# Storing four residual tiles during the routing and keeping expert 6's gate/up weights in their place

## The reference

```
x = x + mixer(rms_norm(x, g_mix))
x = x + hier_moe(rms_norm(x, g_ffn))

gp   = softmax(h @ w_rg + b_rg)            # 4 expert groups, take the best one
e_w  = top-2 of softmax over its 8 experts, normalised, times the group's share
hg, hu = h @ w_gate[e], h @ w_up[e]        # 32 experts, 1024 -> 256
y    = sum_e (silu(hg) * hu * e_w[e]) @ w_down[e]     # 256 -> 1024
```

## Time and profile before

| | us |
|---|---|
| median of 3 runs | 1165.74 (1164.16 to 1169.99) |
| the profiled execution, its own time | 1167.69 |
| its span | 1165.9 |
| matmuls (PE) busy | 1029.6 (88%) |
| SP's largest group of waits: on its own weight loads at L599 | 265.6 in 44 |
| mean TensorE clock granted, of full speed | 0.95 |

### The profile page before, as it was taken

One profiled execution on the slowest core, in us unless ns is written; L12 is line 12 of the kernel. 1 busy time (PEld: TensorE's weight loads), 2 busy tenths in 40 slices (PEclk: granted clock), 3 DMA queues, 4 the chain that ended last, 5 costly groups with the idle time before them and its releaser, 6 DMA issues.

```text
span 1165.9 us, 19198 instructions
## 1 busy us (share of the span) xinstructions
PE 1029.6 (88%) x7043; PEld 652.8 (56%) x7044; DVE 428.8 (37%) x906; ACT 209.6 (18%) x425; POOL 182.5 (16%) x270
## 2 busy tenths in 40 slices
PE   5999998869889988788389989988998999999980
PEld 4888786545555544344167767654555554555540
DVE  2541002454722111111249899635462121211216
ACT  4000102232201110110140101144120111111112
POOL 1000010000042221211103120110004222323220
PEclk9999999999999998898799999999988999999995
DMA  9424033345479999999752100264056999999946
GB/s 360 204 102 159 7 119 74 134 192 215 151 251 408 408 409 409 408 409 411 312 212 74 43 31 1 47 233 185 37 211 198 406 406 402 410 406 396 406 184 232
DMA packets 74512, 281.61 MB, mean 242 GB/s; under 512 B 13182, under 2 KB 13886, under 8 KB 71296
## 3 DMA queue, kind: packets, MB, share of 16 engines
q1 hardware_dynamic: 58192, 253.76, 55.7%
q0 software_dynamic: 11120, 17.89, 4.4%
q10 hardware_dynamic: 5120, 8.87, 2.3%
HBM read 270.75 MB, written 29.65 MB: 258 GB/s over the span
## 4 chain that ended last, share of the span: by engine, by line
PE 62%; DMA 21%; DVE 12%; ACT 2%; issue 2%; SPq 0%; POOLq 0%; DVEq 0%; ACTq 0%; POOL 0%
DMA ring<-w_moe 12%; PE psum L2175 12%; PE psum L2079 7%; DMA ar<-w_moe 6%; PE psum L2242 6%; PE psum L1850 6%; PE psum L1806 5%; PE psum L2281 5%; DVE ar L1709 5%; PE psum L2306 3%; PE psum L1919 2%; PE psum L2158 2%; DVE X L1426 2%; PE psum L2207 1%; DMA ring<-expert_outputs 1%
## 5 line engine op out<-in xcount | busy, mean ns | idle before, releaser
L2175 PE MATMUL psum<-ring,ar 128*64 128x256 f32 x1408 | 176.0, 394 | 21.9 <-DMA ring<-w_moe 15.9
L2175 PEld LDWEIGHTS psum<-ring,ar 128*64 128x64 f32 x1408 | 100.9, 141 | 93.8 <-issue 32.6
L2281 PE MATMUL psum<-ar,ring 128*128 128x272 f32 x512 | 121.3, 398 | 5.3 <-DVE ar L1695 2.9
L2281 PEld LDWEIGHTS psum<-ar,ring 128*128 128x128 f32 x512 | 97.6, 192 | 30.2 <-issue 4.2
L1632 DVE COPY ar<-psum 128x128 f32<-128x128 f32 x64 | 18.7, 291 | 247.8 <-PE psum L2232 247.8
L1709 DVE SCALAR_TENSOR_TENSOR ar<-ar,sv 128x512 f32<-128x512 f32 x120 | 106.9, 893 | 5.8 <-ACT ar L1049 1.9
L2079 PE MATMUL psum<-ring,ar 128*128 128x512 f32 x192 | 90.7, 622 | 4.7 <-DVE ar L1411 4.7
L2175 PE MATMUL psum<-ar 128*64 128x256 f32 x640 | 82.9, 404 | 8.2 <-DMA ar<-w_moe 8.2
L2242 PE MATMUL psum<-ring,ar 128*64 128x512 f32 x352 | 84.1, 598 | 0.8 <-DVE ar L1632 0.8
L2175 PEld LDWEIGHTS psum<-ar 128*64 128x64 f32 x640 | 46.2, 144 | 43.0 <-issue 12.9
L973 ACT ACTIVATE ar<-psum 128x128 f32<-128x128 f32 x64 | 17.8, 278 | 288.9 <-PE psum L2175 288.9
(11 more groups left out here) (265 smaller groups left out, 1205.4 us busy)
## 6 DMA issues: line engine op xcount, KB each, us to landing
ring<-w_moe SPq DMA_DIRECT2D x44, 2048.0 KB, 16.6
ring<-w_moe SPq DMA_DIRECT2D x44, 1024.0 KB, 18.6
ar<-w_moe SPq DMA_DIRECT2D x20, 2048.0 KB, 16.7
ar<-w_moe SPq DMA_DIRECT2D x20, 1024.0 KB, 18.3
ring<-w_pw SPq DMA_DIRECT2D x6, 2048.0 KB, 10.8
ring<-w_mix SPq DMA_DIRECT2D x3, 3072.0 KB, 29.3
ring<-expert_outputs SPq DMA_DIRECT2D x6, 1024.0 KB, 9.1
ring<-kv_in SPq DMA_DIRECT2D x2, 2880.0 KB, 11.1
```

The costliest lines, as they stand in the source:

```text
L2175: t = mm(psum[64 * f:64 * f + 64, u % 2, 0:2 * P], xt[:, k, 64 * (u % 2):64 * (u % 2) + 64], w[:, k, f, :], start=k == 0, stop=k == KD - 1)
L2281: t = mm(psum[:, glu_bank(m) + h, 0:HALF], w[:, k, o:o + P], hT2[:, k, HALF * h:HALF * h + HALF], start=k == 0, stop=k == KD - 1)
```

## The change

Four tiles of `X` (4, 2, 3, 0) are stored to a new buffer in memory as soon as they are normed, by ScalarE's queue. When these stores have landed and TensorE has transposed the tiles, SP loads expert 6's four gate/up pieces into the places of tiles 2, 3, 4 and 0, in two transfers, after the preloads of experts 0 to 5. In the first round of the expert loop ScalarE copies one piece into slot 0 after each of `keep_y(1)` to `keep_y(4)`; the fourth copy increments `w_in[0]` by 16, as the load did. The load of expert 6's gate/up in `weights` is left out. The stored tiles are loaded back behind the last expert's down weights, and `combine` waits for them.

```diff
+        x_dram = nc.dram_tensor("residual_rows", (TOK, D), F32, kind="Internal").ap()
 ...
 # SP, experts(n), after the preloads
+                sp.wait_ge(moe.residual, 160 * n + 64)
+                sp.wait_ge(turned, 10 * (2 * n + 1) + 2 * (TILES - 1))
+                for tiles, c in ((slice(2, 5), 0), (slice(0, 1), 3)):
+                    k = tiles.stop - tiles.start
+                    sp.dma_start(X[:, tiles, :], w_moe[n, MSLOTS, c:c + k, :, :].rearrange("c p x -> p c x")
+                                 ).then_inc(moe.residual, 16)
+
-                def weights(it, jobs):
+                def weights(it, jobs, staged=False):
                     for u in range(jobs):
                         sp.wait_ge(moe.gu_free, MSLOTS * it + (EXPERTS * n + u + 1 - MSLOTS))
                         sp.sem_inc(moe.seen, 1)
                         b = (u - 2) % MSLOTS
                         sp.wait_ge(moe.w_in[b], 16 * it + 16 * (loads_before(n, b) + (u >= 2)))
                         e = bass.ds(MSLOTS * it + u, 1)
-                        sp.dma_start(pieces(u)[:, 0:GU, :], ...).then_inc(moe.w_in[u], 16)
+                        if not staged or u:
+                            sp.dma_start(pieces(u)[:, 0:GU, :], ...).then_inc(moe.w_in[u], 16)
                         sp.wait_ge(moe.down_done, MSLOTS * it + (EXPERTS * n + u + 1 - MSLOTS))
                         sp.sem_inc(moe.seen, 1)
                         sp.dma_start(pieces(u)[:, GU:, :], ...).then_inc(moe.w_down_in[u], 16)

-                with sp.Fori(1, EXPERTS // MSLOTS) as it:
+                weights(1, MSLOTS, True)
+                with sp.Fori(2, EXPERTS // MSLOTS) as it:
                     weights(it, MSLOTS)
                 weights(EXPERTS // MSLOTS, EXPERTS % MSLOTS)
+                sp.wait_ge(moe.w_in[0], 16 * (loads_before(n, 0) + 2))
+                for i in (0, 2, 3, 4):
+                    sp.dma_start(X[0:ROWS[i], i, :], x_dram[P * i:P * i + ROWS[i], :]).then_inc(moe.residual, 16)
 ...
 # ScalarE, norm(call), call odd
                         act.dma_start(xn_dram[P * i:P * i + r, :], xn[0:r, :]).then_inc(moe.xn_out[s % 2], 16)
+                        if s < TILES - 1:
+                            act.dma_start(x_dram[P * i:P * i + r, :], X[0:r, i, :]).then_inc(moe.residual, 16)
 ...
 # ScalarE, experts(n)
+                def unstage(c):
+                    act.wait_ge(moe.gu_free, EXPERTS * n + 1)
+                    act.wait_ge(moe.residual, 160 * n + 96)
+                    t = nc.scalar.activation(slot(0)[:, PIECE * c:PIECE * c + PIECE], X[:, (2, 3, 4, 0)[c], :], ACT.Copy)
+                    if c < GU - 1:
+                        link(t)
+                    else:
+                        t.then_inc(moe.w_in[0], 16)
 ...
                         silu(it, u, first)
                         if later(first, u):
                             keep_y(it, u - 1, first)
+                        if first and u >= 2:
+                            unstage(u - 2)
 ...
 # VectorE
             def combine(n):
+                dve.wait_ge(moe.residual, 160 * n + 160)
```

More of the change, by code:

```diff
@@ L298, in __init__ @@
                 self.combined = sem("combined")
+                self.residual = sem("residual")
         class Further:
@@ L598, in weights @@
                         e = bass.ds(MSLOTS * it + u, 1)
-                        sp.dma_start(pieces(u)[:, 0:GU, :], w_moe[n, e, 0:GU, :, :].rearrange("a c p x -> p (a c) x")
-                                     ).then_inc(moe.w_in[u], 16)
+                        if not staged or u:
+                            sp.dma_start(pieces(u)[:, 0:GU, :],
+                                         w_moe[n, e, 0:GU, :, :].rearrange("a c p x -> p (a c) x")
+                                         ).then_inc(moe.w_in[u], 16)
                         sp.wait_ge(moe.down_done, MSLOTS * it + (EXPERTS * n + u + 1 - MSLOTS))
```

## The result

The changed kernel takes 1202.96 us (median of 6 runs, 1198.09 to 1208.42), the one before 1169.64 in the same comparisons: a ratio of 1.0275, 95% interval 1.0238 to 1.0311, that is 32 us slower. The forecast was 1192 against a before of 1165.74, 26 us slower. The profiled execution spans 1198.8 us, 32.9 more than the one of before.

A forecast was written before the change was run, and what follows sets the result against it. The prediction took layer 0's experts as bound by the DMA engines and layer 1's by TensorE. Its terms 12.4 + 4 + 9.6 made 26.0 us, so 1192 against a median of 1165.74, range 1181 to 1202.

The forecast's parts named there:

- What binds and what holds the stream: Layer 0's experts bound by DMA, layer 1's by TensorE; SP's wait on w_in[0] for ScalarE's fourth copy holds later weight loads.
- Staging wins nothing: Expert weight stream: slots, not bytes, hold its start, so leaving out expert 6's load wins at most 1.5 us, taken as 0.
- Layer 0's experts, 12.4: Expert loop of layer 0: expert 8's load lands late and all later loads keep the distance, +12.4 us.
- The landing I took from the earlier trace as 7.8: Expert 8's gate/up load, issued into an empty queue, takes 7.8 us like expert 6's earlier load.
- The copy, 1.15 in the sum: ScalarE's fourth copy, 128x1024, after keep_y(4): 1.15 us, taken from the scaling of a norm.
- The 6.8 us that follow from the fit: Expert 8's 2.1 MB load by the skill page's fit: 6.8 us, one less than the trace row, which was preferred.
- the queue was to be empty by 353: Layer 0's weight queue: loads issued before the hold are through by some 353, then it is empty until 367.35.
- Layer 0's end, 4: After layer 0's experts: the reload adds 4.2 us to the queue and the read-back starts later, +4 us, bounds 1.5 and 6.
- Layer 1, 9.6: Expert loop of layer 1: the same wait makes expert 8's load 12.8 us late, less 3.2 slack, +9.6, bounds 5 and 13.
- The 1 us for a gather lengthened by the staging: Layer 1's start: expert 6's preload may lengthen GpSimd's gather of the first further chunk, +1 us, bounds 0 and 3.
- What costs nothing: Both layers' stores, the first three copies and layer 1's reload are covered by idle time and cost nothing.
- Expert 6's late start: TensorE starts expert 6 in layer 0 at 367.35 instead of 365.22, +2.1 us, the same 2.1 in layer 1.

The follow-up runs named there:

- e1: Changed kernel, but SP does not wait for the landing of expert 6's gate/up before issuing expert 8's: 1182.68 us, ratio 1.0108.
- e2: Kernel before plus one wait only: SP issues expert 8's gate/up after ScalarE's keep_y(4); no stores, staging or reload: 1196.44 us, ratio 1.0225.
- e6: Kernel before with only the wait before expert 8's gate/up, released one expert earlier, after keep_y(3): 1185.00 us, ratio 1.0124.
- e5: Changed kernel with ScalarE's four copies made after experts 1 and 2, and without SP's wait before expert 8's issue: 1176.40 us, ratio 1.0057.
- e8: Kernel before, unchanged, profiled a second time: 1171.42 us.
- e9: Changed kernel with early copies, no SP wait before expert 8's issue, and layer 0's second w_pw1 load moved behind the read-back: 1171.28 us, ratio 0.9991.
- e7: Changed kernel, but after the hold SP issues expert 8's gate/up alone and goes on only when it has landed: 1204.36 us in one run.
- e3: Changed kernel with SP's wait kept, but ScalarE makes all four copies after experts 1 and 2, two each: 1177.15 us, ratio 1.0054.
- e4: Kernel before plus the stores of four residual tiles, their reload and combine's wait; no staging, copies or hold: 1177.64 us, ratio 1.0067.

## Why the prediction was right, and where its sizes were off

**What binds and what holds the stream: right**, from the code and the earlier trace rows. The load was taken out, its wait was not, and the semaphore behind it moved from a transfer that had landed at 342.3 to ScalarE's fourth copy. e1, e2 and e6 show it from three sides.

**Staging wins nothing: right** (I took 0, e5 gives 0.2 us).

**Layer 0's experts, 12.4: measured 16.4 us** against the first profile, 14.6 against the second. Two terms were too small. The issue of expert 8's load came 43.2 us after expert 0's start where my sum had 40.65, and expert 1 to expert 2 took 9.7 us where the first profile of before had 6.9. Of these 2.8 us the unchanged kernel shows 1.6 in e8 (8.5), so that part belongs to the execution and not to the change; 9.7 was seen only here and in e9, both with staging, while e5, with staging too, has 6.9. The landing I took from the earlier trace rows as 7.8 took 9.1; expert 6's, from which I took it, had no scatter beside it (see e7). The copy, 1.15 in the sum, took 1.05. The page ScalarE: Activation LUTs of the Trainium skill gives 1.04 for it (section What ACT_TABLE_LOAD costs), and the trace agrees. The 6.8 us that follow from the fit on the Trainium skill's page DMA: Bandwidth & Descriptors (section Anatomy of one DMA) the trace does not bear out for this load, which took 9.1. One step of the working that the sum did not use was off too: the queue was to be empty by 353, 26 us after expert 0's start, and ran dry 5 us later than that. Expert 6's down load went out at 343.92, after 2 us without any traffic, and expert 7's landed at 358.68, 31.6 us after expert 0's start.

**Layer 0's end, 4: measured 5.1.** Right in size, wrong in place. I had the read-back starting late in a full queue and called the scatter's delay one that runs beside it. It is the scatter, 7.20 us for 3.72, that moved; the read-back took 7.21 us where it had taken 7.18. The remaining 1.6 are expert 31's products at the lower clock, 4.00 us for 2.38. They come with the long hold: the changed kernel, e2 and e7 have 4.00 to 4.07 there, all other profiles 2.38; why is not shown.

**Layer 1, 9.6: measured 13.5.** The mechanism was as predicted, lateness less a slack of 3.2 us: expert 31 landed 1158.35 - 904.8 = 253.6 us after expert 0's start, before 1122.6 - 885.7 = 236.9, so 16.7 late, and 16.7 - 3.2 = 13.5. Of the 3.9 us between the two, 2.9 are the landing of expert 8's load, 10.7 instead of 7.8, and 1.0 its issue, 43.6 us after expert 0's start instead of 42.6; expert 1 to expert 2 took 8.6 us there, before 6.9. The 1 us for a gather lengthened by the staging is not borne out: e3 has the same staging, and from expert 0 to expert 1 it takes 7.7 us there, e4 without staging 7.7 too, and over all profiles 6.6 to 8.4 without order.

**What costs nothing: right** for layer 1's reload (last two columns of the table). For the stores and the first three copies a cost of a few us could hide in the scatter of the first and fourth column; that there is none beyond some 4 us is shown by e9, which has all of them and stands level. Expert 6's late start did not show in the sum.

The sum was 26.0, the three terms measured make 35.0, and the fourth stretch gave 2.8 back by its clock. Against e8's profile of before the same three terms measure 14.6, 5.0 and 11.4, together 31.0: part of the excess is that the sum started from a profile with expert 1 at full clock. The rest is that all three terms erred the same way, the load's landing in both layers and the slow products behind the hold. The forecast was 1192 within 1181 to 1202. The measured 1202.96 stands beside a before of 1169.64; on the 1165.74 of the forecast the ratio gives 1197.8 (1193.5 to 1202.0), so the value lies in the upper part of the range. The mechanism was right, its size a fifth too small.

## What to carry to other kernels

When a transfer is replaced by a copy on an engine, look for everyone who waits on its semaphore, not only the consumer: here the consumer waited 1.7 us, which the lengths of the expert stretches did not show, and a flow-control wait on the issuing queue lost 26 us. Before taking bytes out of a DMA-bound stream, check whether its start is held by bytes or by slots; the first load's landing against the next one's earliest issue tells. A load's duration should be taken from a place with the same neighbours in the queue, and a difference of 5 us in one profile of this kernel is within what goes with its clock.

## What was not expected

The queue's tail cost time only through the small scatter in front of which it stood: 7.0 to 8.1 us with 1.7 MB more in it, 3.73 once 2 MB were moved behind it (e9), while the 4.5 MB read-back that follows took 7.1 to 7.3 us in layer 0 of all profiles but one (9.4 in e7).

The first 2 MB load behind a hold took 8.6 to 10.7 us, and issuing it alone or with three more behind it made no difference of over 0.3 us (e7).
